# Gate and up of two feed-forwards as seven block products of half-size blocks, in three parts

## The chip, the cores and the metric

The kernel runs on one core of a Trainium2 chip. The metric is the device time of one launch in microseconds. Nothing is computed on the host between input and output.

## What is computed

Two small networks of two layers each over 512 tokens with width 1024: an RWKV-7 layer and an mLSTM layer, each followed by a feed-forward, then a retention layer and a latent-attention layer. All operands are float32. The change touches the two feed-forwards alone:

```python
def _swiglu(x, w_gu, w_down):
    gu = x @ w_gu
    return (jax.nn.silu(gu[..., :D_FF]) * gu[..., D_FF:]) @ w_down
...
    h = _rms(x) * (1.0 + sc2) + sh2
    x = x + g2 * _swiglu(h, ffn_w_gu[i], ffn_w_down[i])
```

`D_FF` is 2816, that is 22 tiles of 128. The six vectors of a layer (`sc2`, `sh2`, `g2` and so on) come from one product of a vector with `ada_w`. The kernel computes them on VectorE from rows of 128 x 1024 weights (`ada_tile`, L672), multiplying and summing in one instruction.

## The kernel before

Activations stand with features on partitions and 512 tokens along the free axis. The float32 product is made of three matmuls with rounded operands (`three`, L348 to L350): high times high, high weights times low activations, low weights times high activations. So each weight block needs a rounded copy, `w_high` (ScalarE, `Split.high`, L369), and a remainder that is written over the block in the ring (GpSimd, `Split.low`, L379). The ring has four slots of 128 x 2048 floats (1 MB), and `w_high` two buffers. SyncE loads block b (L188) when block b - 4 has been used.

`ffn` (L2050) is called once for each layer. Its first product takes 22 blocks, each with one tile of gate and one of up over all eight tiles of the contraction: `pe_first` for the first, following the norm tile by tile, and `pe_features` for the rest, 48 matmuls of 512 columns a block. ScalarE takes silu of the gate bank, VectorE multiplies with the up bank (L2111), ScalarE rounds the result (L2092) and VectorE makes its low part (L2115). Then ScalarE rounds block b + 2 and GpSimd makes its low part. The second product (`pe_long`) takes 16 blocks, two for each tile of the output, 66 matmuls a tile. VectorE adds each tile to `x` (L2143), and `tail` squares it for the next norm.

The order on each engine is the order in which the functions `tensor`, `scalar`, `vector`, `gpsimd` and `sync` issue; there is no scheduler. In layer 0 VectorE also works through 40 rows of the next layer's modulation weights (L672), two behind each of the first 20 blocks, from one buffer that SyncE refills when the row has been used (L2158). The eight rows for `g2` come in two transfers of 2 MB on ScalarE's queue into the place of `h`, once all of the first product is done, and are summed before the first output tile is taken.

The end of a feed-forward overlaps the start of the next phase: ScalarE and GpSimd prepare the next phase's first two blocks (`tail.scalar`, `tail.gpsimd`), the first of them behind `tail.tile_scalar(6)` on ScalarE.

## Time and profile before

| | before |
|---|---|
| three runs, us | 2656.14, 2662.59, 2667.69 |
| median, us | 2662.59 |
| the profiled execution, its span, us | 2659.2 |
| TensorE busy, us | 2502.6 (94%) |
| VectorE busy, us | 1289.9 (49%) |
| ScalarE busy, us | 1006.5 (38%) |
| GpSimd busy, us | 874.2 (33%) |
| DMA, moved | 272.15 MB |

The profiled execution is known by its span, from the first to the last instruction; what lies around that is not in it. PE is TensorE and PEld its weight loads, DVE is VectorE, ACT is ScalarE, POOL is GpSimd, SP is SyncE. A matmul's record lasts longer than the distance to the next, since matmuls are pipelined, so the pace is read from starts. The number behind "idle before" names what an engine last waited for.

### The profile page before, as it was taken

What the parts mean: (1) busy time and instruction counts of PE and PEld (TensorE: products, weight loads), DVE (VectorE), ACT (ScalarE), POOL (GpSimd) and SP (SyncE); (2) the same over time, 40 slices, a digit from 0 to 9 for tenths busy, and PEclk for the clock granted to TensorE, in tenths of its full rate; (3) what the DMA queues carried; (4) which work ended last, traced back from release to release, by engine and by line L of the source; (5) the groups of instructions that cost most, each with busy time, mean ns of one, the idle gap of its engine ahead of it and who ended that gap; (6) DMA issues with size and microseconds to landing.
All of it is one profiled execution on the core that took longest, in us unless ns stands there. A gap on an engine that the chain in (4) does not pass through costs nothing.

```text
span 2659.2 us, 34456 instructions
## 1 busy us (share of the span) xinstructions
PE 2502.6 (94%) x14296; PEld 1997.5 (75%) x14296; DVE 1289.9 (49%) x1893; ACT 1006.5 (38%) x1500; POOL 874.2 (33%) x280
## 2 busy tenths in 40 slices
PE   7996667899999999999999999999999999999999
PEld 5745565578887887878888787899977777777786
DVE  5564885764444254343111434456625625666604
ACT  4652453432322233433322233333334334554523
POOL 2312331314444433453444443423233343111132
PEclk8998898999999999999999999999999999999999
DMA  6121343315555322112222542212122222111121
GB/s 272 64 79 31 92 94 90 128 72 190 189 190 209 131 96 95 48 64 79 95 95 95 190 142 99 95 66 78 64 103 79 93 86 106 55 62 63 56 95 64
DMA packets 92104, 272.15 MB, mean 102 GB/s; under 512 B 54720, under 2 KB 54848, under 8 KB 64320
## 3 DMA queue, kind: packets, MB, share of 16 engines
q1 hardware_dynamic: 89232, 255.03, 27.3%
q10 hardware_dynamic: 2736, 15.21, 1.5%
q8 instruction: 97, 1.59, 0.2%
q14 instruction: 39, 0.32, 0.0%
HBM read 264.44 MB, written 5.78 MB: 102 GB/s over the span
## 4 chain that ended last, share of the span: by engine, by line
PE 79%; DVE 10%; ACT 5%; issue 3%; DMA 2%; POOL 1%; SPq 0%; ACTq 0%; DVEq 0%; POOLq 0%
PE bank L348 20%; PE bank L350 20%; PE bank L349 19%; PE bank L284 2%; PE bank L282 2%; PE bank L283 2%; POOL ring_low L379 1%; DVE q_rope L3689 1%; PE bank L3156 1%; ACT w_high L369 1%; PE bank L3467 1%; PE bank L809 1%; PE bank L2274 1%; PE bank L2299 1%; DVE inv_t L1679 1%
## 5 line engine op out<-in xcount | busy, mean ns | idle before, releaser
L379 POOL TENSOR_TENSOR ring_low<-ring,w_high 128x2048 fp32r<-128x2048 f32 (+2 forms) x174 | 760.5, 4371 | 1482.6 <-ACT w_high L369 1482.6
L348 PE MATMUL bank<-h_high,w_high 128*128 128x512 f32 (+1 forms) x1304 | 520.2, 399 | 5.7 <-POOL ring_low L379 2.8
L350 PE MATMUL bank<-h_high,ring_low 128*128 128x512 f32 (+1 forms) x1304 | 517.2, 397 | 0.0
L349 PE MATMUL bank<-h_low,w_high 128*128 128x512 f32 (+1 forms) x1304 | 514.1, 394 | 0.0
L369 ACT ACTIVATE w_high<-ring 128x2048 fp32r<-128x2048 f32 (+2 forms) x182 | 327.7, 1800 | 354.9 <-PE bank L350 343.0
L348 PEld LDWEIGHTS bank<-h_high,w_high 128*128 128x128 f32 (+1 forms) x1304 | 244.9, 188 | 67.3 <-issue 6.6
L349 PEld LDWEIGHTS bank<-h_low,w_high 128*128 128x128 f32 (+1 forms) x1304 | 244.8, 188 | 59.9 <-issue 0.7
L350 PEld LDWEIGHTS bank<-h_high,ring_low 128*128 128x128 f32 (+1 forms) x1304 | 244.7, 188 | 59.5
L348 PE MATMUL bank<-z_high,w_high 128*128 128x512 f32 x384 | 154.2, 402 | 9.7 <-DVE z_low L1996 3.0
L350 PE MATMUL bank<-z_high,ring_low 128*128 128x512 f32 x384 | 153.2, 399 | 0.0
L349 PE MATMUL bank<-z_low,w_high 128*128 128x512 f32 x384 | 152.9, 398 | 0.0
L2111 DVE TENSOR_TENSOR product<-silu_gate,bank 128x512 f32<-128x512 f32 x44 | 30.2, 687 | 240.7 <-PE bank L350 240.7
L348 PE MATMUL bank<-hidden_high,w_high 128*128 128x512 f32 x352 | 139.6, 397 | 2.3 <-POOL ring_low L379 2.3
L350 PE MATMUL bank<-hidden_high,ring_low 128*128 128x512 f32 x352 | 139.5, 396 | 0.0
L349 PE MATMUL bank<-hidden_low,w_high 128*128 128x512 f32 x352 | 138.6, 394 | 0.0
L672 DVE SCALAR_TENSOR_TENSOR ada_slot<-ada_slot,c_row 128x1024 f32<-128x1024 f32 x56 | 94.1, 1691 | 72.4 <-DMA ada_slot<-in_ada_next 72.4
L2092 ACT ACTIVATE hidden_high<-product 128x512 f32 (+1 forms) x44 | 27.8, 632 | 247.0 <-DVE product L2111 247.0
L282 PE MATMUL bank<-w_high,h_high 128*128 128x256 f32 x384 | 109.7, 286 | 1.1 <-POOL ring_low L379 1.1
L284 PE MATMUL bank<-w_high,h_low 128*128 128x256 f32 x384 | 110.3, 287 | 0.0
L283 PE MATMUL bank<-ring_low,h_high 128*128 128x256 f32 x384 | 109.7, 286 | 0.0
L348 PEld LDWEIGHTS bank<-z_high,w_high 128*128 128x128 f32 x384 | 73.0, 190 | 32.7 <-issue 8.2
L350 PEld LDWEIGHTS bank<-z_high,ring_low 128*128 128x128 f32 x384 | 73.0, 190 | 17.3
(484 smaller groups left out, 4594.0 us busy)
## 6 DMA issues: line engine op xcount, KB each, us to landing
ring<-in_stream SPq DMA_DIRECT2D x194, 1024.0 KB, 4.8
ada_slot<-in_ada_next SPq DMA_DIRECT2D x40, 512.0 KB, 3.3
ada_slot<-in_first SPq DMA_DIRECT2D x8, 1024.0 KB, 5.3
gain_weights<-in_gains ACTq DMA_DIRECT2D x4, 2048.0 KB, 12.5
scale_weights<-in_first SPq DMA_DIRECT2D x4, 1024.0 KB, 19.1
inverse<-scratch_inverse SPq DMA_DIRECT2D x16, 256.0 KB, 4.2
w_first<-in_first SPq DMA_DIRECT2D x2, 1024.0 KB, 7.7
x_res<-in_x SPq DMA_DIRECT2D x2, 1024.0 KB, 12.0
```

What stands on the lines that cost most here:

```text
L282: pe.matmul(out, x_high[:, tok], w_high[:, k, :], start=(k == 0), stop=False)
L283: pe.matmul(out, x_high[:, tok], w_low[:, k, :], start=False, stop=False)
L284: mm = pe.matmul(out, x_low[:, tok], w_high[:, k, :], start=False, stop=(k == kt - 1))
L348: pe.matmul(out, w_high[:, k, cols], x_high, start=start, stop=False)
L349: pe.matmul(out, w_high[:, k, cols], x_low, start=False, stop=False)
L350: return pe.matmul(out, w_low[:, k, cols], x_high, start=False, stop=stop)
L369: act.activation(self.high_buf[:, b % 2, 0:cols], self.c.ring[:, b % SLOTS, 0:cols], ACT.Copy)\
L379: pool.tensor_tensor(self.c.ring_low[:, b % SLOTS, 0:cols], self.c.ring[:, b % SLOTS, 0:cols], self.high_buf[:, b % 2, 0:cols].bitcast(F32 ...
L672: return dve.scalar_tensor_tensor(out=weights, in0=weights, scalar=1.0, in1=chip.c_row[:, :], op0=ALU.mult, op1=ALU.mult, accum_out=chip.m ...
L809: mm = pe.matmul(chip.bank[5 + i % 3][:, j:j + 1], w[:, k, j * P:(j + 1) * P], c_col[:, k:k + 1], start=(k == 0), stop=(k == KD - 1))
L2092: act.activation(at(hid_high, 4 * i + s), one(prod[:, s % 2, :]), ACT.Copy).then_inc(rounded.sem, 1)
L2111: dve.tensor_tensor(prod[:, s % 2, :], silu[:, (u0 + s) % 2, :], chip.pair(u0 + s)[1][:, :], ALU.mult)\
```

## The change

Gate and up of the first four tiles are computed as before, in two blocks (now two tiles of gate and two of up). The other 40 tiles form ten units. A unit has one block of gate and one of up, each with 256 output columns, and takes the contraction in two halves and the tokens in two halves: a product of 2 x 2 blocks by 2 x 2 blocks. By the scheme of Strassen it is made of seven block products, named by their left operand: A11, S1, S2, A12, S3, S4, A22. Four sums of weight blocks are made on VectorE in each unit (`sum1` to `sum4`), and four sums of activation blocks once per layer (`Forms`). The results are combined in four banks: ScalarE copies a bank to seed another (`seed_b`, `seed_c`) and keeps one product (`keep5`), and VectorE adds that to two banks (`join_d`, `join_b`). All seven weight operands are rounded on ScalarE (`Seven.high`), and their low parts are made on VectorE (`Seven.low`). The units use banks 0 to 3 and 4 to 7 in turns.

The feed-forward is cut into three parts with 8, 8 and 6 tiles of hidden features (units 0 to 2 with the first four tiles, 3 to 6, 7 to 9). After each part the second product runs over these features alone, in four blocks of two output tiles, and VectorE adds each output tile to `x` three times per layer in place of once. The low parts of these blocks stay on GpSimd. All modulation rows now come one at a time into two buffers in turns. The counts of rows in the last unit of each part and in the second product of each part are tables (`in_unit`, `in_down`).

```diff
+FF_PARTS = (8, 8, 6)
+FF_UNITS = ((0, 1, 2), (3, 4, 5, 6), (7, 8, 9))
+FF_LOWER = (False, True, False, True, False, True, False, False, True, False)
...
+    in_unit = ((8, 8, 8) if ada_next else (8, 0, 0))
+    in_down = (((2, 2, 2, 2), (3, 3, 3, 3), (4, 0, 0, 0)) if ada_next else ((0,) * 4,) * 3)
...
+    def product(self, pe, d, i, name, fresh):
+        pe.wait_ge(self.rest.sem, self.rest.of(7 * d + i))
+        w_high, w_low, bank = self.high_place(d, i), self.place(d, i, 1), self.bank(d, name)
+        x_high, x_low = self.moving[i]
+        for k in range(self.QUARTER):
+            for j in range(2):
+                cols, out = slice(j * P, (j + 1) * P), bank[:, j * HALF:(j + 1) * HALF]
+                pe.matmul(out, w_high[:, k, cols], x_high[:, k, :], start=fresh and k == 0 and j == 0, stop=False,
+                          skip_group_check=True)
+                pe.matmul(out, w_high[:, k, cols], x_low[:, k, :], start=False, stop=False, skip_group_check=True)
+                mm = pe.matmul(out, w_low[:, k, cols], x_high[:, k, :], start=False, stop=(k == self.QUARTER - 1),
+                               skip_group_check=True)
...
+    def tensor(self, pe, d, free_a, free_d, ready):
...
+        free_a()
+        ready(self.A11)
+        self.product(pe, d, self.A11, "a", True)
+        free_d()
+        ready(self.S1)
+        self.product(pe, d, self.S1, "d", True)
+        pe.wait_ge(self.seeded.sem, self.seeded.of(3 * d))
+        ready(self.S2)
+        self.product(pe, d, self.S2, "b", False)
+        ready(self.A12)
+        self.product(pe, d, self.A12, "a", False)
+        pe.wait_ge(self.seeded.sem, self.seeded.of(3 * d + 2))
+        ready(self.S3)
+        self.product(pe, d, self.S3, "c", False)
+        ready(self.S4)
+        self.product(pe, d, self.S4, "b", False)
+        pe.wait_ge(self.joined.sem, self.joined.of(2 * d))
+        ready(self.A22)
+        self.product(pe, d, self.A22, "c", False)
...
+                if n is None:
+                    take_rows(in_unit[p] // 2)
+                    seven.join_d(dve, d, p5[:, :])
+                    take_rows(in_unit[p] // 4)
+                    seven.join_b(dve, d, p5[:, :])
+                    products(d)
+                    take_rows(in_unit[p] // 8)
+                    low(d, 0)
+                    low(d, 1)
+                    take_rows(in_unit[p] // 8)
+                    continue
...
+            tail.tile_scalar(act, 0)
+            splits[p].high(act, b + 2, cols=cols)
+            tail.tile_scalar(act, 1)
+            tail.tile_scalar(act, 2)
+            splits[p].high(act, b + 3, cols=cols)
+            for n in range(3, KD - 2):
+                tail.tile_scalar(act, n)
+            tail.next().split.high(act, tail.next().b0)
...
     def gpsimd(pool):
-        by_four(pool, KF, lambda i, s: split.low(pool, b0 + s + 2, i))
-        for n in range(2, 2 * KD):
-            split.low(pool, b1 + n, cols=HALF)
+        for p, (b, u) in enumerate(downs):
+            for s in range(4):
+                splits[p].low(pool, b + s, cols=2 * P * FF_PARTS[p])
         tail.gpsimd(pool)
```

In the built program these places read as follows. A row is the source line, the operation, output <- inputs, its shape and the semaphores waited for.

VectorE before, in the first product of layer 0, one block:

```order
L2111 TENSOR_TENSOR product_123<-silu_gate_122,bank 128x512 [waits gemm_done,step13]
L2115 TENSOR_TENSOR hidden_low_125<-product_123,hidden_high_124 128x512 [waits step15]
L672 SCALAR_TENSOR_TENSOR ada_slot_129,mod_54<-ada_slot_129,c_row_55 128x1024 [waits ada_tile_here] x2
```

VectorE in the changed kernel, one unit in the middle of part two (sums at L2098, L2106, L2111 and L2119, weight lows at L2125, joins at L2157 and L2161):

```order
L2098 TENSOR_TENSOR h_118<-ring_50 128x4x256 [waits step4,w_full1,w_full0]
L2106 TENSOR_TENSOR h_118<-h_118,ring_50 128x4x256 [waits step6,step4]
L2111 TENSOR_TENSOR ring_50<-ring_50 128x1024
L2125 TENSOR_TENSOR ring_low_51<-ring_50,w_high_62 128x1024 [waits step8,step6]
L2157 TENSOR_TENSOR bank<-bank,fifth_128 128x512 [waits step4,step5]
L2125 TENSOR_TENSOR h_scratch_121<-h_118,w_high_62 128x4x256 [waits step8,step6]
L2119 TENSOR_TENSOR h_118<-ring_50,h_118 128x4x256 [waits step6,step4]
L2125 TENSOR_TENSOR h_scratch_121<-h_118,w_high_62 128x4x256 [waits step8,step6]
L2161 TENSOR_TENSOR bank<-bank,fifth_128 128x512 [waits step4]
L2125 TENSOR_TENSOR ring_low_51<-ring_50,w_high_62 128x1024 [waits step8,step6]
L2509 TENSOR_TENSOR product_129<-silu_gate_127,bank 128x512 [waits step21,step24,gemm_done]
L2509 TENSOR_TENSOR product_129<-fifth_128,bank 128x512 [waits step21,step24,step7]
```

Where a block of the first product had two narrow instructions of its own on VectorE, a unit now has four sums and seven weight lows of 1024 elements between its joins and products.

VectorE in the changed kernel, the last unit of part two in layer 0:

```order
L672 SCALAR_TENSOR_TENSOR ada_slot_130,mod_54<-ada_slot_130,c_row_55 128x1024 [waits ada_here1]
L2157 TENSOR_TENSOR bank<-bank,fifth_128 128x512 [waits step4,step5]
L672 SCALAR_TENSOR_TENSOR ada_slot_130,mod_54<-ada_slot_130,c_row_55 128x1024 [waits ada_here0]
L672 SCALAR_TENSOR_TENSOR ada_slot_130,mod_54<-ada_slot_130,c_row_55 128x1024 [waits ada_here1]
L2161 TENSOR_TENSOR bank<-bank,fifth_128 128x512 [waits step4]
L2509 TENSOR_TENSOR product_129<-silu_gate_127,bank 128x512 [waits step21,step24,gemm_done]
L2509 TENSOR_TENSOR product_129<-fifth_128,bank 128x512 [waits step21,step24,step7]
L672 SCALAR_TENSOR_TENSOR ada_slot_130,mod_54<-ada_slot_130,c_row_55 128x1024 [waits ada_here0]
L2530 TENSOR_TENSOR hidden_low_126<-product_129,hidden_high_125 128x2x256 [waits step23] x2
```

Rows of modulation weights now stand ahead of and between the joins, the products and the hidden lows of the unit that the second product waits for (three more stand ahead of the first one shown).

## Rows read from the trace of the kernel before

**Rows 1.** The page, busy time: us, share of the span, instructions.
```profile
PE 2502.6 (94%) x14296; PEld 1997.5 (75%) x14296; DVE 1289.9 (49%) x1893; ACT 1006.5 (38%) x1500; POOL 874.2 (33%) x280
```

**Rows 2.** Both feed-forwards by windows: length, busy time and count of each engine, clock, DMA.
```profile
583.00:953.00 370.00, 369.39 (x1591) 298.02 (x1590) 142.65 (x172) 102.93 (x100) 152.00 (x37) 1.00 0.47 173
1219.00:1590.00 371.00, 369.03 (x1584) 297.32 (x1584) 85.73 (x101) 111.08 (x113) 151.29 (x37) 1.00 0.32 116
```

**Rows 3.** Waits of TensorE from 1205 to 1600: us, times, longest.
```profile
PE bank L348 <- POOL ring_low L379: 2.0, 2, 1.6
```

**Rows 4.** Timeline of TensorE, 512-wide: start, us, the first and the 26th.
```profile
600.03 0.39 PE L349 MATMUL bank<-h_low,w_high 128*128 128x512 f32 x1
...
605.84 0.40 PE L350 MATMUL bank<-h_high,ring_low 128*128 128x512 f32 x1
```

**Rows 5.** Timeline of TensorE, 256-wide: the first and the 27th.
```profile
1014.83 0.28 PE L284 MATMUL bank<-w_high,h_low 128*128 128x256 f32 x1
...
1017.92 0.28 PE L283 MATMUL bank<-ring_low,h_high 128*128 128x256 f32 x1
```

**Rows 6.** Groups of VectorE: line, tiles, count, busy us, mean ns, idle before.
```profile
L379 DVE TENSOR_TENSOR ring_low<-ring,w_high 128x2048 fp32r<-128x2048 f32 x5 | 11.4, 2287 | 4.1 <-ACT w_high L369 4.1
...
L2115 DVE TENSOR_TENSOR hidden_low<-product,hidden_high 128x512 fp32r<-128x512 f32 x24 | 16.6, 692 | 21.4 <-ACT hidden_high L2092 21.4
```

**Rows 7.** Timelines of VectorE and GpSimd near 1482.
```profile
1480.64 1.21 DVE L672 SCALAR_TENSOR_TENSOR gain_weights<-gain_weights,c_row 128x1024 f32<-128x1024 f32 x1
...
1482.61 4.07 DVE L672 SCALAR_TENSOR_TENSOR gain_weights<-gain_weights,c_row 128x1024 f32<-128x1024 f32 x1 [0.76 <-DMA gain_weights<-in_gains]
...
1482.38 3.23 POOL L379 TENSOR_TENSOR ring_low<-ring,w_high 128x1408 fp32r<-128x1408 f32 x1 [5.04 <-ACT w_high L369]
```

**Rows 8.** Groups of GpSimd and ScalarE: the weight lows and the rounding.
```profile
L379 POOL TENSOR_TENSOR ring_low<-ring,w_high 128x2048 fp32r<-128x2048 f32 x137 | 637.6, 4655 | 1192.9 <-ACT w_high L369 1192.9
...
L379 POOL TENSOR_TENSOR ring_low<-ring,w_high 128x1536 fp32r<-128x1536 f32 x9 | 31.9, 3549 | 169.0 <-ACT w_high L369 169.0
...
L369 ACT ACTIVATE w_high<-ring 128x2048 fp32r<-128x2048 f32 x142 | 271.1, 1909 | 167.3 <-PE bank L350 156.0 <-DMA ring<-in_stream 7.3 <-ACT y_squares L3182 2.4
```

**Rows 9.** Timeline of VectorE: end of one row of weights, start of the next.
```profile
598.56 0.08 DVE L672 DVE_READ_ACCUMULATOR ada_slot<-ada_slot,c_row 128x1 f32 x1
...
602.33 1.90 DVE L672 SCALAR_TENSOR_TENSOR ada_slot<-ada_slot,c_row 128x1024 f32<-128x1024 f32 x1 [3.69 <-DMA ada_slot<-in_ada_next]
```

**Rows 10.** DMA issues: count, KB each, median us to landing.
```profile
ring<-in_stream SPq DMA_DIRECT2D x194, 1024.0 KB, 4.8
```

**Rows 11.** Timelines at the start of layer 0's feed-forward: TensorE, end of the norm.
```profile
583.66 0.48 PE L348 MATMUL bank<-h_high,w_high 128*128 128x512 f32 x1 [0.28 <-DVE h_low L459]
...
590.69 1.63 DVE L459 SCALAR_TENSOR_TENSOR h_low<-h,mod,h_high 128x512 fp32r<-128x512 f32 x2
```

**Rows 12.** Windows of 1 us (clock third from the end); one pause of TensorE.
```profile
63.00:64.00 1.00, 0.00 (x0) 0.00 (x0) 1.00 (x2) 0.08 (x1) 1.00 (x2) 1.00 0.00 0
...
181.00:182.00 1.00, 1.00 (x4) 0.51 (x4) 1.00 (x2) 0.56 (x2) 0.00 (x0) 0.50 0.00 0
...
2110.00:2111.00 1.00, 0.00 (x0) 0.00 (x0) 1.00 (x1) 0.93 (x1) 1.00 (x1) 1.00 0.56 115
...
2113.00:2114.00 1.00, 1.00 (x4) 0.81 (x3) 1.00 (x1) 0.00 (x0) 1.00 (x1) 0.50 0.09 33
...
2114.00:2115.00 1.00, 1.00 (x4) 0.82 (x4) 1.00 (x1) 0.00 (x0) 1.00 (x1) 0.75 0.00 0
...
2111.48 0.80 PE L348 MATMUL bank<-h_high,w_high 128*128 128x512 f32 x1 [2.56 <-POOL ring_low L379]
```

**Rows 13.** Timelines at the end of layer 1's feed-forward: GpSimd, TensorE.
```profile
1590.43 0.47 PE L348 MATMUL bank<-h_high,w_high 128*128 128x512 f32 x1 [0.26 <-issue]
...
1584.59 4.61 POOL L379 TENSOR_TENSOR ring_low<-ring,w_high 128x2048 fp32r<-128x2048 f32 x1 [4.98 <-ACT w_high L369]
```

**Rows 14.** Rows of modulation weights, layer 0: min/median/max ns, first and last start.
```profile
L672 DVE SCALAR_TENSOR_TENSOR ada_slot<-ada_slot,c_row x40: 1216/1432/2395, 597.4 to 814.7; 128x1024 f32<-128x1024 f32 x40
```

More of the change, by code:

```diff
@@ L2065, in ready @@
             eng.wait_ge(chip.pair_free[u % 2], 2 * (u // 2) + n % 2 + 1)
[L2067 removed]
+        tail = RawTail(chip, low_offset, ready, (lambda n: 1.0, lambda n: chip.v("final_w")[:, n:n + 1]))
+    rows = [(chip.io["gains"][layer, 1, n // 4][:, n % 4, :], m + 40 + n) for n in range(KD)]
     if ada_next:
[L2069 to L2071 removed]
+        rows += [(chip.io["ada_next"][t], 48 + t) for t in range(40)]
@@ new lines, in high, with keep5 @@
+        def high(d, half):
+            act.wait_ge(product.sem, product.of(2 + 2 * d + half))
+            act.activation(hidden_place(hid_high, d, half), product_of(half), ACT.Copy).then_inc(rounded.sem, 1)
+        def keep5(d):
+            act.wait_ge(product.sem, product.of(2 + 2 * (d - 1) + 1))
+            seven.keep5(act, d, p5[:, :])
+        forms.high(act, 0)
+        first_gate(0)
+        for i in range(2):
+            seven.high(act, 0, i)
+        first_high(0)
+        forms.high(act, 1)
@@ new lines, in sync @@
+        for n in range(4):
+            chip.load(sp, b0 + n)
+        sp.wait_ge(chip.phase_done, 4 * phase)
+        for p in range(len(FF_UNITS)):
+            b, _ = downs[p]
+            for n in range(units[firsts[p]] + 2, b + 2):
+                chip.load(sp, n)
+            send_rows(in_unit[p])
+            chip.load(sp, b + 2)
+            chip.load(sp, b + 3)
+            if p + 1 < len(FF_UNITS):
+                send_rows(in_down[p][0] + in_down[p][1])
+                chip.load(sp, b + 4)
+                send_rows(in_down[p][2])
+                chip.load(sp, b + 5)
+                send_rows(in_down[p][3])
+            else:
+                send_rows(sum(in_down[p]))
```

543 lines of the change are left out of this document (450 added, 93 removed).

## The prediction

> **What bounds the kernel now.** I read the page's busy shares, then the two stretches that the change rewrites, then who keeps TensorE waiting there. TensorE is busy 94% of the span [rows 1]. In the two feed-forwards it is busy 369.4 of 370 us and 369.0 of 371 us at full granted clock, while VectorE works 143 and 86 us, ScalarE 103 and 111 us and GpSimd about 152 us [rows 2]. The longest wait of TensorE there is 1.6 us, for a weight low [rows 3]. So a feed-forward lasts as long as its matmuls, and whatever removes matmul time shortens it, as long as the other engines keep up. About half a percent, 13 us, is what a measurement of this kernel can tell from no change.
>
> **Matmul time removed.** Twenty-five 512-wide matmuls start in 5.81 us, 0.2324 us each [rows 4]. Twenty-six 256-wide ones start in 3.09 us, 0.1188 us each [rows 5], a little over half. Four tiles of gate and up took 4 x 8 x 3 = 96 wide matmuls, 22.31 us. A unit takes 7 x 4 x 2 x 3 = 168 narrow ones, 19.96 us (2.85 us a product). That is 2.35 us less, 47.0 us for 20 units. The second product keeps its 528 wide matmuls a layer. Two extra 512-wide matmuls a layer (set_bits) cost 0.9 us in all. The late gain rows of layer 1 no longer cause the 1.6 us wait [rows 3]. Matmuls alone: -47.7 us.
> The Trainium skill (TensorE: Matmul & The Clock Gate, Back-to-back issue gap) speaks against narrow matmuls: it gives a sustained 81 ns at 128 columns and 131 ns at 512. An estimate between them is 98 ns at 256; by that page a unit would take 16.4 us where 12.6 stood, 77 us more in all. The trace does not agree (232.4 and 118.8 ns), and I give that no chance.
>
> **The work that must keep up.** VectorE gets 11 instructions of 1024 elements per unit: four sums and seven weight lows. A 512-wide one takes 0.692 us and a 2048-wide one 2.287 us [rows 6]; on the line between them 1024 takes 1.2 us. With two joins, two products and two hidden lows of 0.69 us a unit costs 11 x 1.2 + 6 x 0.69 = 17.3 us of 19.96. VectorE becomes the bound only above 1.44 us per wide instruction. ScalarE: seven roundings of about 1.0 us (half of 1.91 [rows 8]) and seven instructions of 0.63 us, 11.4 us. It fits too. Ring loads land in 4.8 us [rows 10] and are asked for a unit ahead. In the middle of a part I cost all this at nothing: TensorE hides it. If that cover were gone, each unit would last as VectorE does.
> Where the cover is thin, I walk VectorE's queue in its written order.
>
> **Start of each feed-forward.** TensorE starts at 583.7 and VectorE ends the norm at 592.3 [rows 11]. Two ordinary blocks and set_bits last to 606.5, products A11 and S1 to 612.2. VectorE is held by the second block's product until 606.4, and then has 0.7 + eight 256-wide instructions (0.43 us each on the line of [rows 6]) + sum, form low and weight low of 1.2 us each = 7.7 us before S2 can start: 614.1, a wait of 1.9 us. It then waits for S3 (622.6); join, form low and low hold A22 up by 0.4 us; the three sums and one low of the next unit end at 630.5, where TensorE came at 628.8. About 4 us a layer, **8 us**; bounds 2 and 7 a layer.
>
> **End of part one (both layers).** Count from the first matmul of the last unit. VectorE is 8.8 us behind it. Then stand four rows of 1.22 us before join_d. Two are there; each further slot is refilled only after its row is used, and 3.69 us pass from the end of one row to the start of the next [rows 9]. So the third row runs from 13.7 to 14.9. ScalarE rounds the down block once A12 is done (11.4) and ends at 14.1, and GpSimd's low of 4.65 us [rows 8] then has the turn. VectorE instructions with two operands in SBUF stand still while GpSimd runs: one started at 1482.61, lasted 4.07 us instead of 1.21, and the GpSimd low had run from 1482.38 to 1485.61 [rows 7]. So row four waits to 19.5 and join_d ends at 21.4, where A22 wanted it at 17.1: TensorE waits 4.3 us. The second GpSimd low holds rows five and six to 27.8, join_b follows at 28.5, the products at 29.9, row seven at 31.1, the hidden lows at 32.4. The down product reaches those tiles at 19.96 + 18 x 0.2324 = 24.1. Total 8.3 us, of which the 4.3 is a part; I take **8 us** a layer, 16 in all. Bounds: 4 (rows five and six get in between the GpSimd lows) and 11.
>
> **Parts two and three, layer 0.** Here VectorE is only 6.6 us behind, so join_d is in time (15.1 against 17.1). Row four to six, join_b, products and hidden lows end at 30.3: 6 us of waiting in part two. In part three the lows take 3.55 us [rows 8], the hidden tiles are ready at 27.8 and wanted at 22.7: 5 us. Then the down phases. Part two has 12 rows at 2.45 us (two slots, 3.69 + 1.22) plus about 6 us behind two GpSimd lows: the last ends near 69, and evict, three sums and one low follow to 75. The down product ends at 71: 4 us. In part three four more rows stand before evict 0 (the first lands about 33, behind two ring loads, the last ends about 40), tile_scalar(0) waits for that evict, and the rounding of block b+2 stands behind it on ScalarE: 41 + 1.5 + 3.55 = 46 against 41.8: 4 us. Together **19 us**; bounds 6 and 30.
>
> **Layer 1** has no rows in parts two and three. The hidden low is held by the second GpSimd low: 0.6 and 0.3 us, **1 us**. At its end tiles now come every 18 x 0.2324 = 4.18 us instead of 15.3, and each needs 2.8 us of VectorE, 2.0 us of ScalarE and their hand-overs, with four GpSimd lows in between. tile_scalar(5) slips by about 4 us, to 32.7 of the 33.5 us that the product lasts; the next phase's first rounding stands behind it, and its GpSimd low (which ran 1584.59 to 1589.2, before TensorE began at 1590.43 [rows 13]) ends 5 to 6 us after TensorE is free: **6 us**, bounds 0 and 8. Layer 0's tail: 0.5 us.
>
> **Clock.** After a pause of 2.56 us the granted clock was 0.5 from 2111.5 to about 2114.7 (it is 1.2 GHz instead of 2.4) [rows 12]: 1.6 us lost. Most of my pauses are followed by another one whose end VectorE sets, which swallows this. I add 1 us.
>
> **Sum.** -47.0 - 1.6 + 0.9 + 8 + 16 + 19 + 1 + 6 + 0.5 + 1 = +3.8 us on a span of 2659.2. The median of the three runs, 2662.6, is 3.4 above that span, as what lies around it and the scatter of the runs (11.5) allow. Forecast: 2662.6 + 3.8 = **2666.4 us**, no change that can be told.
>
> **Rivals.**
> *Faster.* All waits come out at their low bounds: VectorE slips in between GpSimd's lows and the rows land in time: 4 at the starts, 8 at the ends of part one, 6 in parts two and three, 1 at the tail, 1 for set_bits, 20 in all; 20 - 48.6 = -28.6, **2634 us**. For it: the 40 rows of layer 0 beside GpSimd took 1.43 us at the median, 1.22 at best and 2.40 at worst [rows 14]. Against: none of them stood behind two lows in a row. Chance 0.28.
> *Slower by the clock.* The place is the matmuls behind each of about 15 waits. Short pauses have left the clock at full (1.5 us at 62.6 to 64.1), but beside ragged work it stood at 0.5 from 176 to 182 [rows 12]. If it also falls behind the 2 us pauses at the starts, or stays for 7 us as there, each pause costs up to 3.5 us, half of which later waits swallow: 15 x 1.75 = 26, **2692 us**. It decides once a pause costs over 0.7 us net. For it: 256-wide products in bursts with waits between. Against: the 3.2 us behind 2111.5. The Trainium skill (TensorE: Matmul & The Clock Gate, A second HAM failure mode: psum-queue depth-cycling) says that small idles between groups of matmuls can let the clock swing; that would be this rival, and [rows 12] bear it out behind the long pause alone. Chance 0.25.
> *Slower by VectorE.* Wide instructions of two operands over 1.44 us each would make VectorE the bound in each unit. At 1.6 us a unit lasts 11 x 1.6 + 4.1 = 21.7 us, 1.8 more: +35 us, **2701 us**. Rows 6 speak against it. Chance 0.05.
>
> **Numbers.** No change 0.42 (forecast), faster 0.28, slower 0.25 + 0.05 = 0.30. The range takes in the low case and most of the clock case: 2634 to 2690. The forecast's own range is 2650 to 2676.
>
> **What would show it.** Inside a unit narrow matmuls should start every 0.119 us and a unit take 20.0 us. TensorE's waits should name join_d's semaphore, the hidden lows, and behind them rows that stand still beside a GpSimd low. VectorE should show 1024-wide instructions of 1.2 us. I am wrong if TensorE's waits in the two feed-forwards sum to under 35 us or over 65, or if the clock is below 0.9 over a whole unit.

## The result and the profile after

| | before | changed |
|---|---|---|
| median of five runs each, us | 2658.4 (2653.3 to 2667.7) | 2678.7 (2673.0 to 2683.1) |
| ratio, 95% interval | | 1.0061 (1.0045 to 1.0078) |
| the profiled execution, its span, us | 2659.2 | 2671.2 |

The change makes the kernel about 0.6% slower, some 16 us by the ratio. The forecast was 2666.4, 3.8 us more than before. The time lies inside the range and beyond the forecast's own range, and on the side that had a chance of 0.30. The two profiled executions differ by 12.0 us, and the phases below add up to that.

The page of the changed kernel, span and busy time, answers to [rows 1]:

```profile
span 2671.2 us, 37741 instructions
PE 2474.6 (93%) x15740; PEld 2049.4 (77%) x15740; DVE 1607.9 (60%) x2219; ACT 1099.0 (41%) x1652; POOL 686.8 (26%) x232
```

Windows from TensorE's first matmul in each feed-forward to about its first one for the next phase (length, then busy time and count of PE, PEld, DVE, ACT and POOL, clock, DMA) answer to [rows 2]:

```profile
583.00:983.00 400.00, 368.92 (x2366) 334.34 (x2367) 307.25 (x343) 154.74 (x182) 63.49 (x14) 0.96 0.42 153
1234.00:1600.00 366.00, 350.64 (x2307) 319.87 (x2308) 241.59 (x262) 158.79 (x190) 56.67 (x14) 0.99 0.31 109
```

In layer 0 TensorE now stands idle for some 30 us and runs at a mean clock of 0.96 where it had 1.00. From first matmul to first matmul, as the timelines of TensorE have them, layer 0's feed-forward takes 397.9 us where it took 378.5: 19.4 more, and my terms for it sum to 9.0. Layer 1's takes 365.8 us to the next phase's first matmul, where it took 371.4: 5.6 less, and my terms sum to -5.2. The mLSTM layer between them has no edit and took 252.9 us in place of 256.9. The rest of the program took 2.2 us more. So the forecast is right for layer 1 and misses 10 us in layer 0.

Waits of TensorE from 570 to 970, layer 0 (us in all, times, longest):

```profile
PE bank L348 <- DVE hidden_low L2530: 11.1, 3, 5.6
PE bank L2175 <- DVE bank L2157: 4.9, 2, 3.2
PE bank L348 <- POOL ring_low L379: 4.6, 1, 4.6
PE bank L348 <- DVE x_res L2536: 4.3, 1, 4.3
PE bank L2175 <- DVE ring_low L2125: 2.1, 2, 1.8
PE bank L2175 <- DVE h_scratch L2125: 1.3, 1, 1.3
PE bank L2175 <- ACT bank L2144: 1.0, 1, 1.0
```

The same from 1200 to 1640, layer 1:

```profile
PE bank L348 <- DVE hidden_low L2530: 5.8, 2, 5.6
PE bank L348 <- POOL ring_low L379: 4.0, 2, 3.5
PE bank L2175 <- ACT bank L2144: 2.5, 1, 2.5
PE bank L2175 <- DVE ring_low L2125: 2.1, 2, 1.8
PE bank L2175 <- DVE h_scratch L2125: 1.3, 1, 1.3
```

[rows 3] had one wait of 1.6 us. Now the hidden lows, join_d (L2157), the output tiles and GpSimd's low of a down block stand there: 29.3 us in layer 0 and 15.7 in layer 1, 45 in all. My terms for waits made 31 and 19.

What stood beside them is the clock. Windows of 2 us behind the wait before part three's second product, and TensorE's row there:

```profile
930.00:932.00 2.00, 0.00 (x0) 0.00 (x0) 1.87 (x5) 0.63 (x1) 0.00 (x0) 0.84 1.00 301
932.00:934.00 2.00, 1.36 (x3) 1.17 (x4) 1.82 (x3) 0.00 (x0) 0.00 (x0) 0.50 1.01 412
934.00:936.00 2.00, 2.00 (x6) 1.52 (x5) 0.00 (x0) 0.00 (x0) 0.00 (x0) 0.50 1.00 422
...
938.00:940.00 2.00, 2.00 (x10) 1.65 (x9) 0.81 (x1) 0.00 (x0) 0.00 (x0) 0.95 0.68 274
...
932.64 0.80 PE L348 MATMUL bank<-hidden_high,w_high 128*128 128x512 f32 x1 [3.69 <-DVE hidden_low L2530]
```

After 3.69 us without a matmul TensorE issues 6 in 2 us instead of 10, at a granted clock of 0.50 (1.2 GHz), until about 938. Added up over windows of 1 us, the clock stood at half for 34.1 us of layer 0's feed-forward (3.4 before) and for 13.6 us from the start of layer 1's to just behind the wait at its end (none before); 3.4 of these come behind that wait. My sum had 1 us for the clock in all. Thus the first reading was that the waits were right and the clock was the miss. The experiments say otherwise.

VectorE, GpSimd and the queue of SyncE in the last unit of part two, whose first matmul starts near 784:

```profile
791.82 1.23 DVE L672 SCALAR_TENSOR_TENSOR ada_slot<-ada_slot,c_row 128x1024 f32<-128x1024 f32 x1 [1.33 <-DMA ada_slot<-in_ada_next]
...
796.34 1.23 DVE L672 SCALAR_TENSOR_TENSOR ada_slot<-ada_slot,c_row 128x1024 f32<-128x1024 f32 x1 [2.05 <-DMA ada_slot<-in_ada_next]
...
798.65 5.21 DVE L672 SCALAR_TENSOR_TENSOR ada_slot<-ada_slot,c_row 128x1024 f32<-128x1024 f32 x1 [1.07 <-DMA ada_slot<-in_ada_next]
...
803.78 0.69 DVE L2157 TENSOR_TENSOR bank<-bank,fifth 128x512 f32<-128x512 f32 x1
804.39 4.98 DVE L672 SCALAR_TENSOR_TENSOR ada_slot<-ada_slot,c_row 128x1024 f32<-128x1024 f32 x1
...
798.17 10.11 POOL L379 TENSOR_TENSOR ring_low<-ring,w_high 128x2048 fp32r<-128x2048 f32 x2 [89.07 <-ACT w_high L369]
...
775.83 8.86 SPq L188 DMA_DIRECT2D ring<-in_stream  x2
784.73 26.14 SPq L2649 DMA_DIRECT2D ada_slot<-in_ada_next  x8
```

SyncE asks for the first row at 784.7, behind two ring loads. It has landed only at 791.8, and the fourth row starts at 798.65, 0.5 us after GpSimd took its turn at 798.17. It takes 5.21 us, and join_d comes behind it. In my walk the two first rows "are there" and join_d is in time.

### The profile page after: what moved, and what is told of

It reads as the page before. It is cut to its first block, busy times and chain, and to the rows that moved or that the text cites. A ratio compares the mean times of both kernels' runs of the same rounds, so it can differ in the third digit from the quotient of the medians.

```text
span 2671.2 us, 37741 instructions
## 1 busy us (share of the span) xinstructions
PE 2474.6 (93%) x15740; PEld 2049.4 (77%) x15740; DVE 1607.9 (60%) x2219; ACT 1099.0 (41%) x1652; POOL 686.8 (26%) x232
## 4 chain that ended last, share of the span: by engine, by line
PE 71%; DVE 14%; ACT 5%; DMA 4%; issue 4%; POOL 1%; SPq 0%; DVEq 0%; ACTq 0%; POOLq 0%
PE bank L348 14%; PE bank L350 14%; PE bank L349 14%; PE bank L2175 4%; PE bank L2177 3%; PE bank L2178 3%; DVE ada_slot L672 3%; DMA ada_slot<-in_ada_next 2%; PE bank L284 2%; PE bank L282 2%; PE bank L283 2%; DVE q_rope L4199 1%; DMA ada_slot<-in_gains 1%; PE bank L3666 1%; POOL ring_low L379 1%
## 5 line engine op out<-in xcount | busy, mean ns | idle before, releaser
L379 POOL TENSOR_TENSOR ring_low<-ring,w_high 128x2048 fp32r<-128x2048 f32 (+1 forms) x126 | 573.0, 4551 | 1683.0 <-ACT w_high L369 1683.0
L369 ACT ACTIVATE w_high<-ring 128x2048 fp32r<-128x2048 f32 (+1 forms) x134 | 247.0, 1848 | 273.8 <-PE bank L350 260.9
L348 PE MATMUL bank<-h_high,w_high 128*128 128x512 f32 (+1 forms) x664 | 267.7, 403 | 9.6 <-POOL ring_low L379 6.1
L350 PE MATMUL bank<-h_high,ring_low 128*128 128x512 f32 (+1 forms) x664 | 264.4, 398 | 0.0
L349 PE MATMUL bank<-h_low,w_high 128*128 128x512 f32 (+1 forms) x664 | 262.9, 396 | 0.0
L348 PE MATMUL bank<-hidden_high,w_high 128*128 128x512 f32 x352 | 145.9, 415 | 25.9 <-DVE hidden_low L2530 17.0
L348 PEld LDWEIGHTS bank<-h_high,w_high 128*128 128x128 f32 (+1 forms) x664 | 125.1, 188 | 43.6 <-POOL ring_low L379 7.2
L350 PEld LDWEIGHTS bank<-h_high,ring_low 128*128 128x128 f32 (+1 forms) x664 | 124.8, 188 | 31.0
L349 PEld LDWEIGHTS bank<-h_low,w_high 128*128 128x128 f32 (+1 forms) x664 | 125.0, 188 | 30.5 <-issue 0.7
L350 PE MATMUL bank<-hidden_high,ring_low 128*128 128x512 f32 x352 | 143.9, 409 | 0.0
L2178 PE MATMUL bank<-h_high,ring_low 128*128 128x256 f32 x480 | 135.2, 282 | 0.0
L2175 PE MATMUL bank<-h_high,extra_high 128*128 128x256 f32 x320 | 91.5, 286 | 5.5 <-DVE bank L2157 4.9
```

The costliest lines, as they stand in the source:

```text
L348: pe.matmul(out, w_high[:, k, cols], x_high, start=start, stop=False)
L349: pe.matmul(out, w_high[:, k, cols], x_low, start=False, stop=False)
L350: return pe.matmul(out, w_low[:, k, cols], x_high, start=False, stop=stop)
L369: act.activation(self.high_buf[:, b % 2, 0:cols], self.c.ring[:, b % SLOTS, 0:cols], ACT.Copy)\
L379: pool.tensor_tensor(self.c.ring_low[:, b % SLOTS, 0:cols], self.c.ring[:, b % SLOTS, 0:cols], self.high_buf[:, b % 2, 0:cols].bitcast(F32 ...
L2175: pe.matmul(out, w_high[:, k, cols], x_high[:, k, :], start=fresh and k == 0 and j == 0, stop=False, skip_group_check=True)
```

## The experiments

All were compared with the kernel before, which ran on the same chip. "Feed-forward 0" and "1" are the distances named above. Half clock is the sum over feed-forward 0. The phases are those of one profiled execution of each kernel. Those of "norows" and "lowst" lie 6.5 and 9.1 us above the median of their runs, that of "combo" 11.3 below.

| kernel | ratio to before (95%) | feed-forward 0, us | 1, us | half clock, us |
|---|---|---|---|---|
| before | 1 | 378.5 | 371.4 | 3.4 |
| changed | 1.0061 (1.0045 to 1.0078) | 397.9 | 365.8 | 34.1 |
| fill | 1.0036 (1.0025 to 1.0047) | 396.0 | 363.6 | 10.2 |
| norows | 0.9937 (0.9917 to 0.9956) | 369.0 | 366.6 | 10.2 |
| behind | 1.0060 (1.0038 to 1.0081) | 404.7 | 357.9 | 41.0 |
| combo | 1.0067 (1.0047 to 1.0087) | 402.4 | 355.1 | 41.0 |
| lows | 0.9969 (0.9949 to 0.9988) | 386.4 | 359.0 | 27.3 |
| spread | 1.0007 (0.9993 to 1.0021) | 380.1 | 365.9 | 17.1 |
| both | 0.9992 (0.9977 to 1.0007) | 378.8 | 362.0 | 17.1 |
| lowst | 0.9994 (0.9979 to 1.0008) | 386.0 | 360.0 | 27.3 |
| best | 0.9918 (0.9900 to 0.9937) | 366.7 | 352.7 | 10.2 |
| bestpool | 0.9944 (0.9925 to 0.9964) | 374.9 | 354.6 | 13.7 |

The distance ends at the first matmul of the next phase, and what is won there need not be kept. The six kernels that round the next phase's first block earlier (combo, spread, both, best, lowst, bestpool) take 1074.5 to 1077.6 us from the end of feed-forward 1 to the end of the span, the other six 1068.7 to 1072.2. Nearly all of the difference arises in the first 40 us of that stretch. TensorE's waits there, for tiles that the next layer's start makes, in "lowst", 1588 to 1630:

```profile
PE bank L3347 <- DVE rho L3494: 2.4, 1, 2.4
PE bank L348 <- DVE h_low L633: 2.3, 1, 2.3
```

In "lows", without that edit, the only wait at this place is one of 1.8 us for GpSimd's low, which belongs to the distance. So some 5 us of the gains in feed-forward 1 of those six come back behind it. Which part of their edits does it was not tried apart.

### Is it the clock? (fill)

TensorE gets matmuls to do in the waits, whose results are thrown away, here ahead of the hidden tiles of the last unit:

```diff
+        def dummies(bank, n):
+            for _ in range(n):
+                pe.matmul(bank[:, :], h_high[:, 7, 0:P], h_high[:, 7, :], start=True, stop=True)
...
+            def before(k):
+                n = ((22, 7, 15) if ada_next else (22, 0, 0))[p]
+                if k == FF_PARTS[p] - 2 and n:
+                    dummies(chip.pair(u + 1)[1], n)
+                pe.wait_ge(rest.sem, rest.of(hidden_of(p, k)))
```

> The changed kernel with its waits left as they are; matmuls of 512 columns whose results are thrown away are issued to TensorE ahead of its longest waits in both feed-forwards (5 to 22 at a place), so that it is busy while it waits. Clock theory (the time lost beyond the waits is granted clock, 34.1 us at half clock in the first feed-forward and 13.7 us in the second): the granted clock goes back to full behind the filled places, half-clock time falls to under 15 us and under 7 us, and the kernel takes 8 to 16 us less than the changed one, about 2662 to 2670 us, or within 0.2% of the kernel before. Rival (the records of the clock are a by-product and the waits alone are the loss): no change to 3 us more, 2678 to 2682 us, since each place is still released by the same semaphore and some of the added matmuls run over.

Its windows over both feed-forwards (columns as above):

```profile
585.00:981.00 396.00, 383.84 (x2468) 346.61 (x2468) 311.01 (x339) 154.12 (x182) 63.18 (x14) 0.99 0.43 155
1235.00:1599.00 364.00, 355.74 (x2340) 323.85 (x2340) 241.66 (x263) 158.91 (x191) 56.88 (x14) 0.99 0.31 110
```

The clock is back at 0.99, and half-clock time fell from 34.1 to 10.2 us and from 13.6 to 6.8. The feed-forwards are shorter by only 1.9 and 2.2 us. By the two ratios the kernel gains 0.25%, about 7 us, with some 5 us of uncertainty either way. The clock theory had 8 to 16, and the rival no gain at all; the runs lie between and do not exclude the lower end of the theory. TensorE at full clock arrives earlier at the next wait, and VectorE, which sets its end, is no earlier. Nor did the added matmuls cost much themselves: in eleven of their twelve places the next real matmul starts within 0.15 us of the semaphore. So the 31 us of half clock given back are worth 4 us by the traces and some 7 us by the runs, and most of layer 0's delay is VectorE's: at a mean clock of 0.99 it is still 17.5 us longer than before.

### What holds VectorE (norows)

The 40 rows for the next layer are left out; their 40 vectors are taken as zero.

```diff
-        rows += [(chip.io["ada_next"][t], 48 + t) for t in range(40)]
+        rows += [(chip.io["ada_next"][t], 48 + t) for t in range(0)]
...
-                    dve.wait_ge(ada_sum.sem, ada_sum.of(len(rows) - 1))
+                    dve.memset(chip.mod[:, 48:88], 0.0).then_inc(cleared.sem, 1)
+                    dve.wait_ge(cleared.sem, cleared.of(0))
```

> The changed kernel without the 40 rows of the next layer's modulation weights in the first feed-forward (they are taken as zero, so what follows computes with other modulation values). Theory (rows in front of join_d, the hidden lows and the first output tile are what TensorE waits for in parts two and three of layer 0): the waits of 3.2 (join_d), 1.8, 4.3, 1.7, 3.7 and 4.6 us go, with the half-clock stretches behind them; the first feed-forward takes 355 to 362 us instead of 378.5 from its first matmul to the next phase, the kernel about 18 us less than the changed one. Rival (GpSimd's weight lows, which stay, hold VectorE and set those waits): the first feed-forward keeps over 370 us.

Feed-forward 0 takes 369.0 us, where 355 to 362 were expected and the rival had over 370. The expectation counted from 378.5 us, which is the kernel before; from the changed kernel's 397.9 it is 28.9 less. By the ratios the kernel takes 1.2% less than the changed one, some 33 us, more than the 18 us expected. TensorE's two longest waits that are left in layer 0 (570 to 970):

```profile
PE bank L348 <- DVE hidden_low L2531: 5.8, 2, 5.6
PE bank L2175 <- ACT bank L2144: 2.6, 1, 2.6
```

The waits for join_d, x_res and block b + 2 are gone. The 5.6 us at the end of part one, behind that part's own eight rows, stay. VectorE's last output tiles of the parts, counted from the first matmul of the phase, end at 142.3, 284.5 and 390.7 us with the rows and at 143.9, 268.5 and 361.8 without. Part one is not faster without its eight rows in the down phase. Part two is 17.6 us faster and part three 12.9, and what is left (124.6 and 93.3 us) is the matmul time: four units and 192 wide matmuls make 124.5, three and 144 make 93.3. So parts two and three cost 30.5 us through their rows, that is through the instructions and the transfers together, which both left here. I had 19.

### Where the rows stand (behind, combo)

In the last unit of a part all rows but two are put behind the hidden lows, and SyncE asks for blocks b + 2 and b + 3 between the rows:

```diff
-                    take_rows(in_unit[p] // 2)
+                    take_rows(min(2, in_unit[p]))
                     seven.join_d(dve, d, p5[:, :])
-                    take_rows(in_unit[p] // 4)
                     seven.join_b(dve, d, p5[:, :])
                     products(d)
-                    take_rows(in_unit[p] // 8)
                     low(d, 0)
                     low(d, 1)
-                    take_rows(in_unit[p] // 8)
+                    take_rows(max(0, in_unit[p] - 2))
```

> The changed kernel with another order on VectorE in the last unit of each part: two rows, both joins, the products, the hidden lows, and only then the other rows; SyncE asks for the two blocks of the second product behind the second and the fourth row. Theory (rows in front of the hidden lows): the waits for hidden_low (5.6 us at the end of part one in both layers, 1.8 and 3.7 us in parts two and three) fall to under 2 us each, the join_d waits of 3.2 and 1.7 us go, the second feed-forward takes 4 to 7 us less, the first 8 to 15 us less; the rows come later and the waits at the first output tiles (4.3 and 4.6 us) stay or grow by up to 3 us. The kernel: 2659 to 2668 us. Rival (GpSimd's low of the down block holds the hidden lows, whatever stands ahead): hidden_low keeps over 4 us at the end of part one and the kernel stays above 2674 us.

The waits for the hidden lows went (0.5 us in layer 0), and in layer 1, which has no more rows than its eight, the feed-forward is 7.9 us shorter. In layer 0 it is 6.8 us longer, where 8 to 15 less were expected. TensorE's waits there, 570 to 990:

```profile
PE bank L348 <- DVE x_res L2536: 16.9, 3, 9.1
PE bank L348 <- POOL ring_low L379: 15.1, 1, 15.1
```

The rows only moved the wait to the output tiles and to block b + 2 of part three, and the kernel, expected at 2659 to 2668 us, took 2678.9. In "combo" the last part takes its first output tile ahead of the rows, and the next phase's first block is rounded one or two tiles earlier.

> The order of the run before, and in the last part the first output tile is taken ahead of the four rows, which then stand between the next tiles; at the end ScalarE rounds the next phase's first block one to two tiles earlier. Theory (each wait is set by the order of rows and roundings, and the clock falls behind each): the 4.6 us wait for block b + 2 in part three and the 3.5 us wait at the end of layer 1 go too, 8 us and their half clock more; the kernel takes 2648 to 2658 us, under the kernel before. Rival (the clock falls for another reason, the narrow matmuls themselves): half-clock time stays at 30 us or more in the first feed-forward though the waits are gone, and the kernel stays above 2662 us.

Layer 1 gains 10.7 us on the changed kernel, layer 0 is still 4.5 us longer, and the kernel is no faster (2678.2 us, where 2648 to 2658 were expected). Both theories missed: the waits did not go, they stand at x_res. For the 20 rows in the last unit and second product of part two, some 64 us, moving them within that stretch alone gained nothing.

### What a row costs beside GpSimd (lows)

VectorE makes the low parts of the second product's blocks itself, rows unmoved. In the scripts of this and the later kernels `r` takes rows, `j` joins, `b` makes the low of a down block, `P` the products, `h` the hidden lows, `e` takes an output tile, `s` and `l` are sums and weight lows of the next unit, `G` and `F` finish the vectors.

```diff
+VECTOR_LOWS = (0, 1, 2)
+IN_UNIT = ['r4 j0 b0 r2 j1 b1 P r1 h0 h1 r1', 'r4 j0 b0 r2 j1 b1 P r1 h0 h1 r1', 'r4 j0 b0 r2 j1 b1 P r1 h0 h1 r1']
...
+            if p in VECTOR_LOWS:
+                continue
```

> The changed kernel with its rows where they are; the low parts of the second product's blocks (four in each part, both layers) are made by VectorE instead of GpSimd, the first two beside the joins, the third behind the second output tile, the last behind the fourth. Theory (in parts two and three of layer 0 the rows wait beside GpSimd's lows, 4.0 to 5.6 us instead of 1.2): a low costs VectorE 2.29 us in place of up to 4.65 us of standing still, the rows of 3.9 to 5.6 us go, the first feed-forward takes 6 to 12 us less than in the changed kernel (397.9), the kernel 2666 to 2674 us. Rival (the rows are slow because each waits for its transfer, 2.45 us a row over two buffers, and the lock only fills time that would be waited anyway): the first feed-forward stays within 3 us of 397.9 and VectorE waits for rows instead.

VectorE's groups of rows and lows in layer 0, first the changed kernel (583 to 982), then this one:

```profile
L672 DVE SCALAR_TENSOR_TENSOR ada_slot<-ada_slot,c_row 128x1024 f32<-128x1024 f32 x48 | 88.2, 1845 | 51.5 <-DMA ada_slot<-in_ada_next 46.2 <-DMA ada_slot<-in_gains 4.9
```

```profile
L672 DVE SCALAR_TENSOR_TENSOR ada_slot<-ada_slot,c_row 128x1024 f32<-128x1024 f32 x48 | 58.4, 1223 | 45.8 <-DMA ada_slot<-in_ada_next 41.9 <-DMA ada_slot<-in_gains 3.6
L379 DVE TENSOR_TENSOR ring_low<-ring,w_high 128x2048 fp32r<-128x2048 f32 x8 | 18.3, 2283 | 0.5 <-ACT w_high L369 0.5
L379 DVE TENSOR_TENSOR ring_low<-ring,w_high 128x1536 fp32r<-128x1536 f32 x4 | 7.0, 1749 | 0.0
```

48 rows took 88.2 us beside GpSimd's lows and 58.4 without: 29.8 us of standing still went, for 25.3 us of lows that VectorE now makes. Rows and lows together keep VectorE busy for 83.7 us, hardly less, but the time falls in other places: feed-forward 0 is 11.5 us shorter, in its range of 6 to 12, and feed-forward 1 6.8. The kernel is now 0.3% faster than before; at 2654.0 us it lies below the 2666 to 2674 expected. The idle time ahead of rows went only from 51.5 to 45.8 us, so the transfers, which the rival blamed, still cost nearly what they did.

That a VectorE instruction with two inputs in SBUF and a GpSimd instruction that reads SBUF contend for an exclusive lock is stated in the Trainium skill (SBUF — State Buffer, "Who interferes with whom"). The trace agrees: a row, which has two such inputs, took 4.98 us beside a GpSimd low of 5.55 us, and 1.22 us alone. Here it was VectorE that stood still, with TensorE behind it.

### Room for the rows (spread, both)

Rows spread over the phase, without and with VectorE's lows. SyncE also asks for rows earlier, and the next phase's first block is rounded earlier. The lines are against the script of "lows":

```diff
-MID_ROWS = {}
+MID_ROWS = {1: 1, 4: 1, 5: 1, 8: 1}
-        take_rows(0)
+        take_rows(4)
         first_product(1)
...
+IN_UNIT = ['r2 j0 b0 j1 b1 P h0 h1 r1', 'r2 j0 b0 j1 b1 P h0 h1 r1', 'r2 j0 b0 j1 b1 P h0 h1 r1']
```

> The changed kernel with its rows of modulation weights spread: 4 in the first two blocks' shadow, one behind units 1, 4, 5 and 8, three in each last unit (one of them behind the hidden lows), 13, 14 and 4 between the output tiles; GpSimd keeps the lows of the second product. The next phase's first block is rounded one or two tiles earlier. Theory (what is lost in layer 0 is room for rows on VectorE at the ends of parts one to three): the waits for join_d and hidden_low go, the first feed-forward takes 380 to 390 us instead of 397.9, the second 5 to 9 us less, the kernel 2655 to 2665 us. Rival (GpSimd's lows hold the rows wherever they stand, as the run that put them behind the hidden lows suggests): the waits move to the output tiles and the first feed-forward stays over 395 us.

> The two edits before together: rows spread, and the lows of the second product on VectorE. Theory: the first feed-forward comes within 6 us of the kernel without the 40 rows (369.0 us), so 369 to 375, the second to 354 to 358 us, and the kernel to 2636 to 2646 us, 0.5 to 1% under the kernel before, the clock over 0.97 in both. Rival (the transfers of rows, 2.45 us each over two buffers, bound VectorE): over 380 us for the first feed-forward, the kernel not under 2650 us.

Feed-forward 0 came to 380.1 us in "spread", with GpSimd's lows, in its range. VectorE's idle time ahead of rows fell from 51.5 to 25.9 us, so the earlier requests have a share in it that was not measured apart from the places. Feed-forward 1, at 365.9 us, gained nothing where 5 to 9 were expected; it has a wait of 10.8 us for h_scratch at its start. "Both" reached 378.8 and not 369 to 375, and layer 1 got worse than with the lows alone (362.0 against 359.0). The kernel took 2659.7 us, not 2636 to 2646. The longest wait of "both" in layer 0 (560 to 980), and VectorE's rows that caused it:

```profile
PE bank L2175 <- DVE h_scratch L2125: 8.0, 1, 8.0
```

```profile
606.72 1.22 DVE L672 SCALAR_TENSOR_TENSOR ada_slot<-ada_slot,c_row 128x1024 f32<-128x1024 f32 x1
...
611.80 1.23 DVE L672 SCALAR_TENSOR_TENSOR ada_slot<-ada_slot,c_row 128x1024 f32<-128x1024 f32 x1 [2.71 <-DMA ada_slot<-in_gains]
...
614.73 0.68 DVE L2516 TENSOR_TENSOR product<-fifth,bank 128x512 f32<-128x512 f32 x1
```

VectorE reaches that place only at 606.7, not at about 597 as I had read from the kernel before, because forms, sums and lows of unit 0 stand ahead. Four rows over two buffers then last to 614.7. The third and fourth wait for their transfers.

### A version that is faster than both (best, lowst, bestpool)

"Best" puts one row there, more rows in the last units, the second down low behind the hidden lows, and no rows between the next unit's sums and lows:

```diff
+IN_UNIT = ['r3 j0 b0 j1 r1 P h0 h1 b1', 'r3 j0 b0 j1 r1 P h0 h1 b1', 'r3 j0 b0 j1 r1 P h0 h1 b1']
+IN_DOWN = ['r2 G e0 e1 b2 r4 e2 r2 e3 b3 r3 e4 s1 s2 s3 e5 l0 l1 s4 e6 r2 e7', 'r1 e0 r2 e1 b2 r2 e2 r2 e3 b3 r4 e4 s1 s2 s3 e5 l0 l1 s4 e6 r2 e7', 'r1 e0 r1 e1 b2 r1 e2 r1 e3 b3 r1 e4 F e5 e6 e7']
+SENDS = [[2, 0, 1, 0, 0, 0, 3, 2, 2, 3], [5, 3, 0, 0, 0, 0, 1, 0, 2, 3, 2, 4], [4, 3, 0, 0, 0, 0, 2, 3]]
```

`SENDS` is the number of rows that SyncE asks for ahead of each ring load, so that a row is asked for as soon as its buffer is free.

> As the run with both edits, but with one row instead of four ahead of the second block's product (where VectorE turned out to be busy until 606.7), two more in each last unit, the low of the second block behind the hidden lows, and no row between the sums and weight lows of the next unit. Theory (the 8.0 us waits for h_scratch at the start of both feed-forwards were the four rows, and nothing else is lost): the first feed-forward takes 370 to 376 us (378.8 before), the second 353 to 357 us, the kernel 2640 to 2652 us. Rival (40 rows beside 7 wide instructions a unit don't fit on VectorE wherever they stand): waits of over 3 us come up at the first units of parts two and three, and the first feed-forward stays at 378 us or more.

Its page, its windows over both feed-forwards, and the waits of TensorE that are left in layer 0 (570 to 950):

```profile
PE 2465.3 (94%) x15740; PEld 2043.1 (78%) x15740; DVE 1606.6 (61%) x2243; ACT 1099.2 (42%) x1652; POOL 580.1 (22%) x208
```

```profile
582.00:949.00 367.00, 357.76 (x2359) 327.26 (x2360) 295.53 (x352) 154.03 (x181) 9.12 (x2) 0.99 0.47 167
1207.00:1560.00 353.00, 347.53 (x2307) 318.14 (x2308) 248.73 (x268) 153.37 (x184) 4.62 (x1) 1.00 0.32 111
```

```profile
PE bank L2175 <- DVE x_res L2543: 2.7, 1, 2.7
PE bank L2175 <- DVE ring_low L2125: 2.5, 3, 1.8
...
PE bank L2175 <- DVE h_scratch L2125: 1.3, 1, 1.3
PE bank L2175 <- ACT bank L2144: 1.0, 1, 1.0
```

The median is 2638.5 us beside 2662.8 for the kernel before, 0.8% faster, and some 38 us faster than the changed kernel by the ratios. It and both feed-forwards came out just below their expected ranges. All 48 rows are in it, and feed-forward 0 is even 2.4 us shorter than "norows" with 40 rows left out. So rows and transfers can stand where they cost far less than in the changed kernel. VectorE is busy as long as in the changed kernel. What changed is the order of its work, that it and not GpSimd makes the lows, and when the rows are asked for.

"Lowst" stands between: the rows of "lows", with the low of the second down block behind the hidden lows (script `r4 j0 b0 r2 j1 r1 P h0 h1 b1 r1`) and the earlier rounding of the tail.

> As the run with the second product's lows on VectorE, with the low of the second block behind the hidden lows, one row less ahead of them, and the next phase's first block rounded a tile or two earlier. Theory (hidden_low, waited for with 9.1 us, is held by a 2.3 us low and a row that can stand behind): hidden_low's waits in the first feed-forward fall under 4 us, that phase takes 380 to 384 us (386.4), the second 355 to 358 us (359.0), the kernel 2645 to 2652 us. Rival (rows wait for their transfers, so what is moved comes back at the next place): within 2 us of 2654.

Its rival held for feed-forward 0: hidden_low fell to 7.5 us, VectorE's own ring_low rose from 5.0 to 9.0, and feed-forward 0 stayed at 386.0. The median of 2660.2 us lies outside what either foresaw, and the ratio is even 0.25% above that of "lows", whose ten runs scattered from 2642.8 to 2666.9 us. The traces have a likely place for it: from the end of feed-forward 1 to the end of the span "lowst" took 1077.6 us and "lows" 1068.9, as told under the table, though the profiled execution of "lowst" is its slowest. "Bestpool" is "best" with the lows of the second product given back to GpSimd.

> The best version so far (rows spread, first feed-forward 366.7 us) with one thing put back: the lows of the second product are made by GpSimd again, everything else in its place. Theory (VectorE's rows stand still beside GpSimd's lows, 4 to 5.6 us instead of 1.2, so that each low costs VectorE more than the 2.29 us that it takes to do it itself): the first feed-forward takes 8 to 14 us more, 375 to 381 us, the second 1 to 5 us more, the kernel 2650 to 2658 us. Rival (the places of the rows were all, and the engine of the lows doesn't matter once they have room): the first feed-forward stays under 370 us and the kernel under 2644 us.

```profile
L672 DVE SCALAR_TENSOR_TENSOR ada_slot<-ada_slot,c_row 128x1024 f32<-128x1024 f32 x48 | 69.9, 1470 | 37.5 <-DMA ada_slot<-in_ada_next 34.0 <-DMA ada_slot<-in_gains 3.5
```

The rows take 69.9 us again in place of 58, feed-forward 0 takes 8.2 us more and feed-forward 1 1.9 more, as the theory had it; the kernel, at 2650.0, lies 0.26% over "best", which is no more than the uncertainty of the two ratios together. So in layer 0 the places of the rows, with the earlier requests and the earlier rounding, are worth more (397.9 to 374.9 us) than the engine of the lows on top of them (374.9 to 366.7). Taken alone, the lows gave 11.5 us ("lows"), so the two do not simply add up.

## Why the prediction was partly right

**Matmul time: right.** At full granted clock wide matmuls of the changed kernel's second product start 0.233 us apart and narrow ones 0.118 us, as in [rows 4] and [rows 5] to within 1%, and parts two and three without rows last as long as their matmuls by the paces of those rows to within 0.1 us. So -47.0 us stood. The first and the 27th narrow matmul of a stretch in the changed kernel:

```profile
743.64 0.28 PE L2178 MATMUL bank<-h_high,ring_low 128*128 128x256 f32 x1
...
746.71 0.28 PE L2177 MATMUL bank<-h_low,w_high 128*128 128x256 f32 x1
```

**VectorE's wide instructions: right.** They took 1.22 us where I put 1.2, and the rival that needed over 1.44 us is out. The Trainium skill (VectorE: DVE Perf Modes, "The TRN2 errata") gives (N + 151)/0.96 ns for an addition of two tensors, by estimate 1224 ns at 1024 columns; the trace agrees.

**Starts of the feed-forwards: right.** 4.1 us in layer 0 (1.3 for h_scratch, 1.8 for ring_low, 1.0 for ScalarE's seed) and 5.6 in layer 1, where 4 each stood.

**End of part one: right in size, wrong at join_d.** 8 us a layer stood, 4.3 of them at join_d. join_d was in time, since its four rows ended at 666.8 and GpSimd began at 666.90. The hidden lows waited 5.6 us in both layers, behind a row of 5.62 us beside GpSimd. In layer 0 evict 7 ended at 142.3 us, where matmuls alone would give 128.0: 14.3 us over, with 12 forecast.

**Parts two and three of layer 0: the step that failed.** The term of 19 us measured 30.6: the 17.7 us and 12.9 us by which the parts exceed their matmuls. I had counted that the first two rows are there when VectorE comes. SyncE's queue, which the sum owed a term, sends them behind two ring loads. The first came 7 us later, at 791.82, and VectorE waited 1.33 us for it. With that the fourth row missed GpSimd's start by 0.5 us and stood still. So join_d was late by 3.2 us where I had it in time. No run asks for the rows earlier and changes nothing else, so the share of the requests in the 30.6 us stays open. The same came again in the down phases, where rows of 4.75 and 4.90 us stand in front of output tiles, and TensorE waited for x_res (4.3 us) at the fourth block, not at the part's end. The waits in TensorE's own rows, 29.3 us, look like the 31 forecast only since TensorE was slowed in between, and so that agreement is luck. With the clock restored ("fill") layer 0 stays 40.6 us over its matmuls, and with it as it was, 42.5 (19.4 + 23.5 - 0.4 for set_bits). The parts, each taken to its last output tile, sum to 44.9, 2.4 more. Half of that is that the next phase starts 7.2 us behind the last tile where it was 8.4; the rest is not explained.

**The clock: mis-sized, and smaller than it looks.** I had 1 us. The half-clock time of 34.1 + 13.6 us suggests 24 us; giving 31 us of it back was worth 4 us in the profiled executions and about 7 in the runs. My condition for that rival was a net price of over 0.7 us a pause. By the same 15 pauses it was 0.3 to 0.5, and 0.4 to 0.7 in proportion, had all of it come back: under the condition, by the runs only just. My other condition, a clock below 0.9 over a whole unit, was not met: the lowest, with one half-clock stretch of 3.4 us in 20, is 0.915.

**Layer 1: right.** One term, its tail, was 3.5 us where 6 stood, and ScalarE's seed added 1.5 that I had not.

**What no term covers:** the mLSTM layer, 4.0 us shorter with no edit in it. Over the kernels of this study it took 252.9 to 258.4 us, a tenth of a percent of the kernel either way. This is the clock: it stood at half there for 17.1 us before, 6.8 in the changed kernel and 20.5 in "best". Windows over the layer in the first two (columns as above):

```profile
962.10:1219.00 256.90, 252.35 (x1373) 207.97 (x1373) 124.24 (x225) 109.45 (x189) 109.33 (x59) 0.97 0.19 70
981.10:1234.00 252.90, 247.86 (x1372) 204.70 (x1373) 124.61 (x225) 109.50 (x189) 109.56 (x59) 0.99 0.20 71
```

Over all twelve kernels the layer is longer by 0.4 us for each us at half clock, to within 0.4 us. TensorE is busy nearly throughout this layer, so most of the half is lost. In the feed-forwards "fill" gained only 0.13 us for each us given back: there VectorE ended the next wait anyway.

## What to carry to other kernels

When work is moved onto an engine that is not the bound, count where the engine becomes the bound for a few microseconds, not its busy share: "best" and the changed kernel keep VectorE equally busy and differ by 38 us. An instruction that can wait (a row for the next layer) should stand behind every one that TensorE waits for, and its transfer should be asked for in the queue before the loads that wait longer (in "best" both were done together). Before blaming the clock for what comes after waits, fill the waits: if another engine ends the next one, the clock's loss was already paid.

## What was not expected of the hardware

- The pause of 1.8 us ahead of unit 1 was followed by about 3.4 us at half clock in the changed kernel and in "best", and by none in "lows". A pause of 2.72 us in "best" was followed by none. TensorE's row and the windows of 1 us around it:

```profile
722.89 0.39 PE L2175 MATMUL bank<-forms_high,w_high 128*128 128x256 f32 x1 [2.72 <-DVE x_res L2543]
...
723.00:724.00 1.00, 1.00 (x9) 1.00 (x10) 1.00 (x2) 0.00 (x0) 0.00 (x0) 1.00 0.81 287
724.00:725.00 1.00, 1.00 (x11) 1.00 (x10) 1.00 (x1) 0.00 (x0) 0.00 (x0) 1.00 0.49 135
```

  So the length of a pause alone does not tell whether the clock falls. What else does was not tried.
- VectorE gets in between two GpSimd lows, one row at a time: rows of 5.21 and 4.98 us, with a join of 0.69 us on a bank between them, beside two lows of 4.61 and 5.55 us. The join itself, which has one operand in a bank, was not held up: it ran from 803.78, within the second low (802.73 to 808.28).
- A layer without an edit moved by up to 5.5 us between the kernels, in step with the half-clock time in it.
